# A gather schedule: two value rows in each quarter up to the 68th and one up to the 128th, in place of one and a half throughout

## What is computed

```
q = (hf @ w_pq).reshape(n, PEER_HEADS, 2, PEER_DHALF)
...
sv, si = lax.top_k(s, PEER_TOPK)
...
u = jnp.take(u_tab, ec, axis=0)
act = jax.nn.gelu(jnp.einsum('cd,ced->ce', hc, u).astype(jnp.float32), approximate=False)
wgt = (gc * act).astype(hc.dtype)
vr = jnp.take(v_tab, ec, axis=0)
return jnp.einsum('ce,ced->cd', wgt, vr)
```

## Time and profile before

| what | value |
|---|---|
| median of the runs | 1992.36 us (1988.22 to 1995.3) |
| the profiled execution's own time | 1991.84 us |
| its span in the profile | 1989.4 us |
| PE busy | 1354.3 us, 68% |
| DVE busy | 1252.0 us, 63% |
| POOL busy | 1094.6 us, 55% |
| ACT busy | 589.5 us, 30% |
| moved by DMA | 701.83 MB, mean 353 GB/s |

### The profile page before, as it was taken

One profiled execution on the slowest core, in us unless ns is written; L12 is line 12 of the kernel. 1 busy time (PEld: TensorE's weight loads), 2 busy tenths in 40 slices (PEclk: granted clock), 3 DMA queues, 4 the chain that ended last, 5 costly groups with the idle time before them and its releaser, 6 DMA issues.

```text
span 1989.4 us, 23567 instructions
## 1 busy us (share of the span) xinstructions
PE 1354.3 (68%) x7318; PEld 873.8 (44%) x7318; DVE 1252.0 (63%) x3037; ACT 589.5 (30%) x1653; POOL 1094.6 (55%) x1062
## 2 busy tenths in 40 slices
PE   6998999857879677988878777444443444544344
PEld 5887799745646445666655544111110111111111
DVE  3265436477788888866667756656667666666640
ACT  2446424233245245222223323112112212211110
POOL 0100000256665556765666767777777777677774
PEclk9999999978989889889989888556566666765667
DMA  9755346699999988999999999999999999999997
GB/s 366 261 176 206 108 159 200 217 382 370 396 349 407 343 324 328 385 409 370 408 407 409 409 407 396 400 409 404 403 407 401 408 403 402 381 409 408 390 402 292
DMA packets 202443, 701.83 MB, mean 353 GB/s; under 512 B 22568, under 2 KB 32368, under 8 KB 202032
## 3 DMA queue, kind: packets, MB, share of 16 engines
q0 software_dynamic: 149760, 545.33, 70.0%
q1 hardware_dynamic: 52560, 155.02, 21.3%
HBM read 691.26 MB, written 11.06 MB: 353 GB/s over the span
## 4 chain that ended last, share of the span: by engine, by line
DMA 20%; issue 14%; POOL 14%; PE 8%; DVE 3%; POOLq 0%; ACT 0%; DVEq 0%; ACTq 0%
DMA arena<-in_v_tab,pku 14%; POOL arena L2153 14%; DMA arena<-in_u_tab,pku 6%; PE y L1149 5%; PE acc L796 2%; DVE arena L1990 1%; PE acc L936 1%; POOLq L2149 0%; DVE pku L2011 0%; PE acc L833 0%; DVE pk L2010 0%; PE turned L1132 0%; DVE pku L2027 0%; DVE arena L1611 0%; DVE pk L2026 0%
## 5 line engine op out<-in xcount | busy, mean ns | idle before, releaser
L1149 PE MATMUL y<-arena 128*32 128x512 f32 x2080 | 413.8, 909 | 495.9 <-DMA arena<-in_v_tab,pku 495.8
L2153 POOL DMA_INDIRECT arena<-in_u_tab,pku x520 | 551.7, 1061 | 344.9 <-issue 156.3
L2153 POOL DMA_INDIRECT arena<-in_v_tab,pku x520 | 527.9, 1015 | 294.0 <-issue 149.1
L796 PE MATMUL acc<-arena 128*128 128x264 f32 (+1 forms) x2304 | 547.4, 395 | 17.4 <-ACT arena L1259 7.8
L796 PEld LDWEIGHTS acc<-arena 128*128 128x128 f32 x2304 | 445.4, 196 | 122.5 <-issue 49.7
L1990 DVE CUSTOM_DVE_ANT_0 arena<-arena,h_bank 128x1024 f32<-128x1024 f32 x240 | 290.8, 1218 | 254.1 <-DMA arena<-in_u_tab,pku 253.3
L1149 PEld LDWEIGHTS y<-arena 128*32 128x32 f32 x2080 | 81.8, 143 | 728.2 <-issue 723.5
L1990 DVE CUSTOM_DVE_ANT_0 arena<-arena 128x1024 f32<-128x1024 f32 x280 | 335.2, 1221 | 84.7 <-DMA arena<-in_u_tab,pku 72.4
L1486 ACT ACTIVATE pk<-pk 128x1 f32<-128x1 f32 x520 | 103.5, 281 | 2.1
L1504 ACT CAST pku<-turned 128x8 uint32<-128x8 f32 x64 | 10.3, 160 | 293.6 <-PE turned L1133 293.6
L1132 PE MATMUL turned<-arena 128*128 128x256 f32 x128 | 58.2, 545 | 55.5 <-DVE arena L2068 55.4
(11 more groups left out here) (249 smaller groups left out, 1873.5 us busy)
## 6 DMA issues: line engine op xcount, KB each, us to landing
arena<-w_mod SPq DMA_DIRECT2D x48, 512.0 KB, 6.2
arena<-w_pq SPq DMA_DIRECT2D x32, 512.0 KB, 7.1
arena<-w_xr SPq DMA_DIRECT2D x20, 512.0 KB, 9.0
arena<-w_qk SPq DMA_DIRECT2D x20, 512.0 KB, 7.0
arena<-w_gr SPq DMA_DIRECT2D x20, 512.0 KB, 6.5
arena<-w_rnn SPq DMA_DIRECT2D x16, 640.0 KB, 7.1
arena<-in_u_tab,pku POOLq DMA_INDIRECT x520, 8.0
arena<-in_v_tab,pku POOLq DMA_INDIRECT x520, 7.8
```

The source lines that it names most:

```text
L796: mm = pe.matmul(a[:, 0:n], w[:, k, :], rhs[:, k, 0:n], start=(k == 0), stop=(k == ks - 1))
L1149: mm = pe.matmul(y[rows, h, :], spread[g % NTURN][:, 32 * j:32 * j + 32], rows_v[j][:, h * 512:(h + 1) * 512], start=first and (g != SAMPL ...
L2153: pool.indirect_dma_start(out=row, out_offset=None, in_=table, in_offset=bass.IndirectOffsetOnAxis(ap=idx, axis=0), **more).then_inc(signa ...
```

## The change

The number of V rows that should have been gathered by quarter k is a straight line of 1.5 per quarter from quarter 10 to quarter 128 before. It becomes a line of 2 per quarter from the 10th to the 68th, and of 1 per quarter from there to the 128th.

```
-V_EARLY, V_LAG = 1.5, 10
+V_FIRST, V_SECOND, V_LAG, V_TURN = 2.0, 1.0, 10, 68
...
     while done < V_SLOTS:
-        early = V_EARLY * max(0, min(k, window) - V_LAG)
-        late = (V_SLOTS - V_EARLY * (window - V_LAG)) * max(0, k - window) / (U_QUARTERS + V_LAG + 1 - window)
+        early = V_FIRST * max(0, min(k, V_TURN) - V_LAG) + V_SECOND * max(0, min(k, window) - V_TURN)
+        before = V_FIRST * (V_TURN - V_LAG) + V_SECOND * (window - V_TURN)
+        late = (V_SLOTS - before) * max(0, k - window) / (U_QUARTERS + V_LAG + 1 - window)
         known = SLOT * ((k - V_LAG) // PARTS + 1) if k >= V_LAG else 0
         goal = min(int(early + late), known, V_SLOTS, done + 4)
```

## The result

The changed kernel takes 1980.47 us (median of 4 runs, 1977.45 to 1982.93) where the kernel before takes 1992.74 in the same comparison. The ratio is 0.9945, with a 95% interval of 0.9929 to 0.9961: faster by 0.55%, or 11 us (the two medians are 12 us apart), and clear of zero. 1978 was predicted. The profiled execution took 1980.11 us, its span is 1978.2 us.

What follows compares the result with a forecast made beforehand. Transfers were taken to bind the kernel from 799 us on, with spare DMA time only before. Span 1989.4 - 13 - 3 + 1.3 = 1974.7 us, 1977.1 with time outside it, 0.5 more for the median: 1978 us; range 1963 to 2003.

Steps and rivals of the forecast that it cites:

- The bound, and where time was to be had: Whole kernel: transfers bind from 799 us to the end; spare DMA time, 26 us, only in the first stretch.
- 10 fewer gathers are worth 13 us there: Behind product 301, the end of attention: 10 gathers moved ahead of it, at 1.3 us each, save 13 us.
- the DMA share is 1.01 already, so these waits are hidden behind the queue: Second part, quarters 70 to 128: shorter POOL waits gain nothing, since transfers are already full.
- should mostly go: Second part: POOL's waits of 30.3 us for PE and 15.0 us for indices would mostly vanish.
- if the queue ran dry there: Second part: the case in which the POOL waits costed at nothing would come back as time; no size given.
- third sign of being wrong: Second part: not shortening despite fewer gathers would mean that PE and not the queue is its bound.
- I take it 3 us shorter: First part: between 13 us shorter if DVE alone set the pace and 11 us longer if PE did.
- The end: From quarter 139 on: one V gather more is left for the last stretch, costing 1.3 us.
- The V loop: First part: V gathers waiting on half-sums and turned indices set the pace; slower, about 1998 to 2012 us; chance 0.22.
- the rival's threshold: First part, V gathers: from stalls of 3.6 us a group on, the change is a loss.
- The limit of some 358 GB/s for one core's share: First stretch, at 361 GB/s, would be full already, so no gain, 1992 us; next to no chance.
- the second rule weighed: POOL's gather issues: DVE's fast modes lock GpSimd out of a shared port; 10 gathers of 0.2 us, 2 us.

Runs made afterwards that it cites:

- e1: The change's line mirrored: 1 V row a quarter from the 10th to the 68th, 2 from there to the 128th; 2021.66 us, ratio 1.0157 to the kernel before.
- e2: V gathers as in the changed kernel, dense products shared over the quarters as before the change; 1970.82 us, ratio 0.9899 to the kernel before.
- e3: V gathers as before the change, dense products shared as in the changed kernel; 1998.55 us, ratio 1.0040 to the kernel before.
- e7: The changed kernel with each group's turn one quarter earlier in the program; 1973.37 us, ratio 0.9911 to the kernel before.

## Why the prediction was right, and where its terms were not

**The bound, and where time was to be had.** Right. Transfers bind the kernel behind attention and leave gaps ahead of it. e1, e2 and e3 move gathers across that line in both directions, and the second part follows them with 1.0 to 1.5 us for each (e2 1.0, e3 1.2, e1 1.5), where 1.3 was taken.

**"10 fewer gathers are worth 13 us there."** Right in kind, but 8 and not 10 gathers left the second part by the trace, and it got 0.1 us shorter and not 13. The 10 were counted up to product 301, which is a `gr`; up to `gate_r`, product 303, reached with quarter 70 before and 66 after, the tables give 210 and 224 gathers, 14 more. The trace has 213 and 220, since POOL does not keep step with PE: at the cut it begins quarter 72 before and 66 after. The step that failed is the one that cost the waits of the second part at nothing, "the DMA share is 1.01 already, so these waits are hidden behind the queue". They were hidden only while the queue was full. With 3 gathers a quarter it was less so, and POOL's stall for turned indices emptied it: the share fell to 1.00, and in e7, without that stall, the part is 10.8 us shorter. Of the two waits that "should mostly go", the one for half-sums did (30.3 us before, 4.4 us after, from 800 to 1150 us), the one for indices did not: the 14.9 us alone are as much as the 15.0 before. The prediction had named this case ("if the queue ran dry there"), without a price. Its third sign of being wrong did come true, the second part did not shorten, but what it was to mean did not: PE is as busy in e7 (329.70 us, 332.27 in the change), and there the part does shorten. PE mattered by the place of the turn in its order, not by its load.

**"I take it 3 us shorter"**, for the first part. It was 6.1 us shorter. DVE's 17 us less work is shown, with 141 dot products in place of 150. That it was what shortened the part is supported by e3, where the same dense shares with the old gathers give 371.7 us against 388.6, about half of which is what 21 gathers fewer are worth. A rival stays open: PE's waits for DVE's turns also fell, and no run moves them alone. Waits of PE in the first stretch, before and then after the change:

```profile
PE turned L1132 <- DVE arena L2068: 36.0, 5, 12.4
```

```profile
PE turned L1133 <- DVE arena L2069: 9.3, 2, 6.9
```

**The cost of the moved dense products.** Here the prediction saw one side. It took the fewer quarters ahead of `gate_r` as DVE's relief and had the gathers that go with them inside its net of 10, but did not ask what they cost alone. By e2 and e3 the moved dense products are a loss on the whole: `gate_r` and what follows come 4 quarters earlier in the tables, 6 by POOL's place at the cut, which takes 12 U and 9 V gathers from beside the first part in e3, and these cost the second part 24.2 us where the first part gains 16.9.

**The end**: 1.3 us more were expected from quarter 140 on, 1.6 us less came. Both are below what one profile can tell. With 3.4 us of scatter ahead of quarter 11 this brings the total nearer to the forecast than its terms were: -7.8 us by the change's own parts, -14.7 forecast. That 1980 lies so near to 1978 is therefore luck in part: 13 us that did not come in the second part were partly made up by 3 more in the first, 3 at the end and the scatter.

**The rivals.** The V loop: POOL's idle time ahead of V gathers did grow in the first stretch, from 64.7 us for 88 to 100.1 for 107 (a V gather waits for a half-sum or for indices; what is put down to DVE is not to be taken by its name):

```profile
L2154 POOL DMA_INDIRECT arena<-in_v_tab,pku x107 | 119.5, 1117 | 100.1 <-DVE pk L1991 37.1 <-issue 28.2 <-PE y L1150 24.2
L2154 POOL DMA_INDIRECT arena<-in_u_tab,pku x106 | 115.3, 1087 | 37.1 <-issue 30.7 <-DVE pk L1991 4.6 <-PE acc L797 1.3
```

Less 107 gaps of 0.30 us that is 68 us, 5.2 us for each of 13 groups, well above the 3.6 us from which the prediction called the change a loss. But the waits ahead of U gathers shrank from 78.1 to 37.1 us at the same time. The stall moved from the U gathers to the V gathers and did not add up, as if POOL waited for the other engines' place in the program either way. So the rival's threshold was wrongly built, though its outcome was rightly held to be unlikely. The limit of some 358 GB/s for one core's share (the Trainium skill, "DMA: Bandwidth & Descriptors", Specifications) does not bind this kernel, which runs on one core alone: the first part went from 360 to 375 GB/s with the change, and to 385 in e2. Whether DVE's instructions lengthen POOL's issues, the second rule weighed, no run tests.

## What to carry to other kernels

Where a long run of transfers is beside a part with other limits, count the transfers that stand beside that part and not the waits of the engine that issues them; here each gather moved to beside the attention part cost 0.4 us there and spared 1.0 us behind it, until the gaps were full. When one table drives two things, try each alone: of this change the moved gathers were worth 21 us and the dense products that followed them cost 6 to 10. A wait hidden by a full queue has to be priced again once the change makes the queue thinner, and what shows its price is the share of the transfers at that place, not the sum of idle time of the engine that issues them.

## What was not expected

PE's place for the half-sum has a sharp edge on one side only. One quarter earlier costs 52 us, one quarter later, for the gathers up to quarter 99, 3 us, with an interval that meets that of the change. A median landing of some 10 us is longer than the one quarter of 6 to 7 us that the early place allows, and PE holds up all dense work while it waits.
